# Gate and up matmuls from rounded halves, 384 columns at once, with rows stored modulated and the down step in two banks

## What is computed

```python
x = x + g1[:, None, :] * (mixed @ w_out[l])
h2 = modulate(rms_norm(x, norm2_g[l]), sh2, sc2)      # h * (1 + scale) + shift
x = x + g2[:, None, :] * hier_moe(h2, ...)
return rms_norm(x, final_g)
...
def expert_block(args):                               # 32 experts, two of them for each row
    tok, e = args
    xb = h_pad[tok]
    a = jax.nn.silu(xb @ w_gate[e]) * (xb @ w_up[e])  # 1024 -> 256
    return a @ w_down[e]                              # 256 -> 1024
```

## Time and profile before

| | us |
|---|---|
| three runs | 1996.19, 1997.77, 1998.21 (median 1997.77) |
| the profiled execution | 1996.46 |
| its span, first to last instruction | 1994.3 |
| TensorE busy | 1801.4 (90%) |
| VectorE busy | 1179.6 (59%) |
| ScalarE busy | 855.5 (43%) |
| mean granted TensorE clock | 0.950 of full speed |

### The profile page before, as it was taken

How to read it: one execution, slowest core, us unless ns; L and a number is a source line. 1 busy time by engine, 2 the same in 40 slices (tenths; PEclk the granted TensorE clock), 3 DMA queues, 4 the chain that set the end, 5 groups by cost and what they waited for, 6 DMA issues and landing times. The chain is left out here.

```text
span 1994.3 us, 26932 instructions
## 1 busy us (share of the span) xinstructions
PE 1801.4 (90%) x8988; PEld 1479.5 (74%) x8988; DVE 1179.6 (59%) x2009; ACT 855.5 (43%) x1520; POOL 855.5 (43%) x887
## 2 busy tenths in 40 slices
PE   2899999997999999999995999965999999999980
PEld 2677878774777777777784788855899898999970
DVE  4597989857666666666644656553444444444444
ACT  3535454326676777677684232311222222222114
POOL 0032314103888888888892111112343443434330
PEclk8899999996999999999997999976999999999995
DMA  7656565530000000000005343414888787878848
GB/s 282 197 143 192 168 181 158 147 102 0 6 9 6 9 8 6 9 9 6 11 9 199 126 158 137 148 43 163 248 248 252 231 248 245 248 236 239 242 94 337
DMA packets 216176, 274.28 MB, mean 138 GB/s; under 512 B 28469, under 2 KB 176144, under 8 KB 215834
## 3 DMA queue, kind: packets, MB, share of 16 engines
q1 hardware_dynamic: 193498, 220.59, 34.1%
q0 software_dynamic: 20224, 52.47, 10.4%
q10 hardware_dynamic: 2368, 0.17, 0.1%
HBM read 229.13 MB, written 60.82 MB: 145 GB/s over the span
## 5 line engine op out<-in xcount | busy, mean ns | idle before, releaser
L1212 POOL TENSOR_TENSOR plo<-KR,phi 128x512 fp32r<-128x512 f32 (+1 forms) x320 | 353.1, 1123 | 44.6 <-ACT KR L1171 44.4
L1020 DVE TENSOR_REDUCE cmax<-tbank 128x1 f32<-128x512 f32 (+2 forms) x320 | 193.3, 605 | 106.8 <-PE tbank L835 101.6
L1170 ACT ACTIVATE phi<-tbank 128x512 fp32r<-128x512 f32 (+1 forms) x320 | 170.9, 534 | 141.8 <-PE tbank L884 137.3
L387 PE MATMUL pbank<-hhi,wslhi 128*128 128x512 f32 x512 | 207.7, 406 | 8.5 <-DVE wsllo L440 8.5
L1946 DVE TENSOR_SCALAR xTe<-ebank,modcol 128x256 f32<-128x256 f32 (+1 forms) x128 | 53.6, 471 | 262.2 <-PE ebank L1864 137.8
L387 PE MATMUL pbank<-hhi,wsllo 128*128 128x512 f32 x512 | 201.5, 394 | 0.0
L387 PE MATMUL pbank<-hlo,wslhi 128*128 128x512 f32 x512 | 201.4, 393 | 0.0
L331 POOL DMA_DIRECT2D wmod<-in_w_ada x64 | 48.5, 758 | 308.2 <-DVE macc L519 297.9
L1886 PE MATMUL ebank<-xTe,wg 128*128 128x192 f32 x1024 | 174.8, 330 | 3.1 <-DVE ahi L1979 1.8
L1886 PEld LDWEIGHTS ebank<-xTe,wg 128*128 128x128 f32 x1024 | 170.9, 193 | 8.0 <-DVE ahi L1979 2.1
L1886 PE MATMUL ebank<-xTe,wu 128*128 128x192 f32 x1024 | 171.6, 326 | 0.0
(11 more groups left out here) (279 smaller groups left out, 3963.4 us busy)
## 6 DMA issues: line engine op xcount, KB each, us to landing
wg<-in_w_exp_gate SPq DMA_DIRECT2D x32, 1024.0 KB, 5.5
wu<-in_w_exp_up SPq DMA_DIRECT2D x32, 1024.0 KB, 8.9
wd<-in_w_exp_down SPq DMA_DIRECT2D x32, 1024.0 KB, 5.0
wraw<-in_w_in SPq DMA_DIRECT2D x60, 512.0 KB, 4.4
wmod<-in_w_ada POOLq DMA_DIRECT2D x64, 256.0 KB, 3.5
xt<-in_x SPq DMA_DIRECT2D x4, 2048.0 KB, 11.4
wada<-in_w_ada SPq DMA_DIRECT2D x4, 2048.0 KB, 19.7
mixed<-mix_dram SPq DMA_DIRECT2D x16, 512.0 KB, 4.3
```

The lines of the kernel that those rows point to most:

```text
L387: ins = pe.matmul(out, w[:, S % 3, k], h[:, n % 2, k], start=k == 0 and j == 0, stop=k == KD - 1 and j == 2)
L1020: W(ve.tensor_reduce(cmax[:, i % 2, n:n + 1], plain[:, chunk % 2, 0:w], AX.X, ALU.max), plain_read)
L1170: A(act.activation(step_of(phi, m), scores[:, m % 2, j * P:512], ACT.Exp), phi_done)
L1212: po.tensor_tensor(step_of(plo, m), step_of(probs, m), step_of(phi, m).bitcast(F32), ALU.subtract).then_inc(plo_done, 1)
```

## The change

Gate and up now also run on halves. ScalarE rounds each half of `wg` and `wu` to `ghi` (8 blocks of 128 columns, four such operations an expert), and VectorE subtracts it to `glo` (four of 1024 columns). The raw weights have one buffer each (`gu[:, 0]`, `gu[:, 1]`). The transposed rows are stored as two halves side by side: ScalarE copies the high one from PSUM, VectorE subtracts the rest. For each block TensorE multiplies `ghi` by both halves at once, 384 columns, and adds `glo` by the high half, 192 columns. So a bank holds two parts, which have to be added: ScalarE copies the low part, VectorE adds the other (`add_gate`, `add_up`, 384 columns each), and Silu then works from SBUF. Gate and up take four banks, so the down step has two: `down_first` and `down_rest` use the same two in turn, and outputs are scaled in halves of 512 columns. The low half of `wd` is made by VectorE, as before.

The rows `xs` are now stored with scale and shift applied (two operations of 1024 columns in place of one). The row vectors for this come from three broadcast loads of 512 KB on ScalarE's queue, four matmuls of 512 columns and three operations of VectorE; the one-column matmuls, the scaled router weights and the router's bias step go. The last stage scales each tile in place and stores two tiles (1 MB) at a time.

```diff
-                ve.tensor_scalar(xs[:, b], x2[:, b], xstat[:, b, 2:3], None, ALU.mult).then_inc(xs_ready, 1)
+                ve.scalar_tensor_tensor(xs[:, b], x2[:, b], xstat[:, b, 2:3], scrow[:], ALU.mult, ALU.mult
+                                        ).then_inc(xs_scaled, 1)
+                ve.wait_ge(xs_scaled, t + 1)
+                ve.tensor_tensor(xs[:, b], xs[:, b], shrow[:], ALU.add).then_inc(xs_ready, 1)
...
+            act.dma_start(shrow[:], b_ada[0, 3 * D:4 * D].partition_broadcast(P)).then_inc(ld_srow, 16)
+            act.dma_start(scrow[:], b_ada[0, 4 * D:5 * D].partition_broadcast(P)).then_inc(ld_srow, 16)
+            act.dma_start(xs[:, 1], T["norm2_g"][0, :].partition_broadcast(P)).then_inc(ld_srow, 16)
...
-        xT = sb("xTe", [P, KD, 2 * CAP])
+        xT = sb("xTe", [P, KD, 2, 2 * CAP], F32R)
...
-        wg, wu, wd = sb("wg", [P, 2, KD, FE]), sb("wu", [P, 2, KD, FE]), sb("wd", [P, 2, KF, D])
+        gu, wd = sb("gu", [P, 2, KD, FE]), sb("wd", [P, 2, KF, D])
+        ghi, glo = sb("ghi", [P, 2, KD, FE], F32R), sb("glo", [P, 2, KD, FE], F32R)
...
-        turn, gate, up, outa, outb = bank[:, 0:2], bank[:, 2], bank[:, 3], bank[:, 4:6], bank[0:CAPB, 6:8]
+        turn, gate, up, outp = bank[:, 0:2], bank[:, 2:4], bank[:, 4:6], bank[:, 6:8]
...
+            def load_gate(r, i, g):
+                sp.wait_ge(glo_ready, r * (NEXP * 4) + i * (NGRP * 4) + (g * 4 + 2))
+                sp.dma_start(gu[:, 0], wgd[:, bass.ds(i * KD + g * EPG * KD, KD), :]).then_inc(ld_g, 16)
+
+            def load_up(r, i, g):
+                sp.wait_ge(glo_ready, r * (NEXP * 4) + i * (NGRP * 4) + (g * 4 + 4))
+                sp.dma_start(gu[:, 1], wud[:, bass.ds(i * KD + g * EPG * KD, KD), :]).then_inc(ld_u, 16)
+
+            def load_down(r, i, g):
+                sp.wait_ge(dlo_ready, r * NEXP + i * NGRP + (g + 1))
+                sp.dma_start(wd[:, g % 2], wdd[:, bass.ds(i * KF + g * EPG * KF, KF), :]).then_inc(ld_wd[g % 2], 16)
...
-                        sp.wait_ge(up_done, r * NEXP + i * NGRP + (g + 1))
-                        sp.dma_start(wg[:, b], wgd[:, bass.ds(i * KD + g * EPG * KD, KD), :]).then_inc(ld_gu[b], 16)
-                        sp.dma_start(wu[:, b], wud[:, bass.ds(i * KD + g * EPG * KD, KD), :]).then_inc(ld_gu[b], 16)
-                        sp.wait_ge(dlo_ready, r * NEXP + i * NGRP + (g + 1))
-                        sp.dma_start(wd[:, b], wdd[:, bass.ds(i * KF + g * EPG * KF, KF), :]).then_inc(ld_wd[b], 16)
+                        load_up(r, i + (g + 1) // NGRP, (g + 1) % NGRP)
+                        load_down(r, i + (g + 1) // NGRP, (g + 1) % NGRP)
+                        load_gate(r, i + (g + 2) // NGRP, (g + 2) % NGRP)
...
-                for w, out, done in ((wg, gate, gate_done), (wu, up, up_done)):
+                pe.wait_ge(turn_dve, r * (PAIRS * 6) + q * 6 + (6 + b * 2))
+                for m, (out, free) in enumerate(((gate, gate_added), (up, up_added))):
+                    pe.wait_ge(free, r * NEXP + q * 2 + (b + 1))
                     for f in range(KF):
+                        pe.wait_ge(glo_ready, r * (NEXP * 4) + q * 8 + (b * 4 + m * 2 + f + 5))
+                        at, both = slice(f * P, (f + 1) * P), out[:, f, 0:2 * CAP].rearrange("p (h n) -> p h n", h=2)
                         for k in range(KD):
-                            ins = pe.matmul(out[:, f * CAP:(f + 1) * CAP], w[:, b, k, f * P:(f + 1) * P],
-                                            xT[:, k, cols_of[b]], start=k == 0, stop=k == KD - 1)
-                    ins.then_inc(done, 1)
-
-            def down(out, b, lo, hi, done):
+                            pe.matmul(both, ghi[:, m, k, at], xT[:, k, :, cols_of[b]], start=k == 0, stop=False)
+                            ins = pe.matmul(both[:, 0], glo[:, m, k, at], xT[:, k, 0, cols_of[b]],
+                                            start=False, stop=k == KD - 1)
+                        ins.then_inc(unit_done, 1)
...
+            def down(n, b, lo, hi, done):
+                out = outp[0:hi - lo, n]
                 for f in range(KF):
                     for j, (a, w) in enumerate(((ahi, dhi), (alo, dhi), (ahi, dlo))):
-                        for n in range(2):
-                            ins = pe.matmul(out[:, n], a[:, b, f, lo:hi], w[:, b, f, n * 512:(n + 1) * 512],
-                                            start=f == 0 and j == 0, stop=f == KF - 1 and j == 2)
+                        ins = pe.matmul(out, a[:, b, f, lo:hi], w[:, b, f, n * 512:(n + 1) * 512],
...
-                pe.wait_ge(ya_done, r * NEXP + q * 2 + (b + 1))
-                down(outa, b, b * CAPB, b * CAPB + P, down_a)
+                for n in range(2):
+                    pe.wait_ge(yb_done, r * (NEXP * 2) + q * 4 + (b * 2 + n + 1))
+                    down(n, b, b * CAPB, b * CAPB + P, down_a)
 
             def down_rest(q, b, r):
-                pe.wait_ge(yb_done, r * NEXP + q * 2 + (b + 1))
-                down(outb, b, 0 if b else P, CAPB if b else CAP, down_b)
+                for n in range(2):
+                    pe.wait_ge(ya_done, r * (NEXP * 2) + q * 4 + (b * 2 + n + 2))
+                    down(n, b, 0 if b else P, CAPB if b else CAP, down_b)
...
+            def split_in(q, b, r, m, f):
+                ve.wait_ge(ghi_ready, r * (NEXP * 4) + q * 8 + (b * 4 + m * 2 + f + 1))
+                at = slice(f * P, (f + 1) * P)
+                ve.tensor_tensor(glo[:, m, :, at], gu[:, m, :, at], ghi[:, m, :, at].bitcast(F32), ALU.subtract
+                                 ).then_inc(glo_ready, 1)
+
+            def add_gate(q, b, r):
+                ve.wait_ge(low_copied, r * (NEXP * 2) + q * 4 + (b * 2 + 1))
+                ve.tensor_tensor(sg[:], sg[:], gate[:, :, 0:CAP], ALU.add).then_inc(gate_added, 1)
...
-                ve.wait_ge(down_b, r * NEXP + q * 2 + (b + 3))
-                ve.wait_ge(st_yb[b], r * (PAIRS * 16) + q * 16)
-                ve.scalar_tensor_tensor(yb[:, b], outb.rearrange("p a n -> p (a n)"),
-                                        gate_b[:, bass.ds(r * 0 + q * 2 + b, 1)], g2row[0:CAPB], ALU.mult, ALU.mult
-                                        ).then_inc(yb_done, 1)
+                for n in range(2):
+                    ve.wait_ge(down_b, r * (NEXP * 2) + q * 4 + (b * 2 + n + 5))
+                    if n == 0:
+                        ve.wait_ge(st_yb[b], r * (PAIRS * 16) + q * 16)
+                    at = slice(n * 512, (n + 1) * 512)
+                    ve.scalar_tensor_tensor(yb[:, b, at], outp[0:CAPB, n], gate_b[:, bass.ds(r * 0 + q * 2 + b, 1)],
+                                            g2row[0:CAPB, at], ALU.mult, ALU.mult).then_inc(yb_done, 1)
...
+            def split_in(q, b, r, m, f):
+                if f == 0:
+                    hold(act, ld_u if m else ld_g, r * (NEXP * 16) + q * 32 + (b * 16 + 16), passed)
+                act.wait_ge(unit_done, r * (NEXP * 4) + q * 8 + (b * 4 + m * 2 + f + 1))
+                at = slice(f * P, (f + 1) * P)
+                act.activation(ghi[:, m, :, at], gu[:, m, :, at], ACT.Copy).then_inc(ghi_ready, 1)
...
-            for t in range(NT):
-                sp.wait_ge(normed, t + 1)
-                sp.dma_start(out_rows[t * P:(t + 1) * P, :], res[:, t % NR]).then_inc(st_out[t % NR], 16)
-            for r in range(NR):
-                sp.wait_ge(st_out[r], 16 * NT // NR)
+                    "(p q) d -> p q d", p=P)).then_inc(ld[i], 16)
+            for i in range(NL):
+                sp.wait_ge(normed, 2 * i + 2)
+                sp.dma_start(out_rows[2 * i * P:(2 * i + 2) * P, :].rearrange("(p q) d -> p q d", p=P),
+                             x2[:, 2 * i:2 * i + 2]).then_inc(st_out, 16)
...
-                if t >= NR:
-                    ve.wait_ge(st_out[t % NR], 16 * (t // NR))
-                ve.scalar_tensor_tensor(res[:, t % NR], x2[:, t], stat[:, t, 2:3], fgrow[:], ALU.mult, ALU.mult
+                ve.scalar_tensor_tensor(x2[:, t], x2[:, t], stat[:, t, 2:3], fgrow[:], ALU.mult, ALU.mult
```

More of the change, by code:

```diff
@@ L1398, in step, with modulation_rows @@
                     turn_x(t - 1, 1 - b)
-                if at == 1:
-                    pe.wait_ge(rbias_read, 1)
-            def modulation_rows(piece, first):
+            def modulation_rows(piece, first, to):
                 pe.wait_ge(ld_macc[piece], 16)
                 for n in range(2):
-                    ins = pe.matmul(turn[:, n], cst[:, C_ONE:C_ONE + P], macc[:, first + n], start=True, stop=True)
+                    ins = pe.matmul(to[:, n], cst[:, C_ONE:C_ONE + P], macc[:, first + n], start=True, stop=True)
                 ins.then_inc(mod_summed, 1)
[L1408 to L1417, removed]
-                    ins = pe.matmul(logit_bank, shift[:, k], wr[:, k], start=k == 0, stop=k == KD - 1)
-                ins.then_inc(rbias_done, 1)
             tiles(pe, step)
@@ L2037, in _ @@
                 n = 5
```

(31 more changed lines are left out.)

260 lines of the change are left out of this document (159 added, 101 removed).

## The result

The changed kernel is slower: 2008.86 us (median of nine runs, 2002.32 to 2011.83) against 1997.99 for the kernel before beside it; the ratio is 1.0053, with a 95% interval of 1.0043 to 1.0063. The prediction was 1941 us, 1926 to 1978. The profiled execution has a span of 2006.5 us, 12.2 more than before.

| place in the program | before, us | after, us | difference |
|---|---|---|---|
| start to the first gate matmul | 1382.2 | 1433.8 | +51.6 |
| from there to the last scaled output of the experts | 555.8 | 518.3 | -37.5 |
| from there to the end | 56.3 | 54.4 | -1.9 |

A forecast was written before the change was run, and what follows sets the result against it. TensorE was taken to bound the expert stage, VectorE close behind. Gate and up -61.4, waits +6, first and last pair +1, mixing 0, last stage -2 sum to -56.4 us: 1941 us, range 1926 to 1978.

The forecast's parts named there:

- The mixing stage: Stage before the experts: one more 1024-column VectorE operation a tile, hidden by TensorE; cost 0, ends -4 and +6 us.
- a mixing stage over 6 us longer: Named sign that the forecast is wrong: the stage before the experts growing by over 6 us.
- rival C: Expert stage: weights land later than 10.4 us, VectorE waits; 1972 us at 11.4, 2053 at 14; chance .11, .06 slower.
- Rival D: Expert stage: the new VectorE subtractions cost more than 1.228 us; at 2.0 the kernel takes 2025 us; chance .05.
- Gate and up: Expert stage: a wide and a narrow matmul take .177 + .0875 us, an expert 8.48 instead of 10.40; -61.4 us.
- rival A: Expert stage: weight loads .11 us apart bind, .287 us a pair of matmuls; gain 39 us, total 1958; chance .10.
- the +6 of waits: Expert loop: TensorE and VectorE wait for each other, .4 us a pair of experts over TensorE's sum; +6 us over 15 turns.
- VectorE: Expert loop: 29.4 us of work a pair of experts against TensorE's 30.6, busy 27 to 30; waits cost +6 us.
- Loads: Expert stage: single raw buffers leave time for a 10.4 us landing, longest median was 8.2; cost nothing.
- the sign that was named for rival C: Expert stage: ScalarE's rounding of gate weights waits for the load, VectorE for ScalarE, with a landing above 10 us.
- The last stage: Final stage: tiles written in place and stored 1 MB at a time; -2 us, ends -3 and +1.3.

The follow-up runs named there:

- the order mended: Changed kernel with VectorE's two small operations for the next tile's scale moved ahead of the two 1024-column operations on the stored row: 1947.46 us, ratio 0.9754 to before.

## Why the prediction was wrong, step by step

- **The mixing stage, forecast 0 (-4 to +6), was +51.6 up to the first gate matmul.** This is the step that failed, and it alone turned the sign. The sentence was: VectorE is busy 151 of 270 us, TensorE 245, "so TensorE hides it". A busy share over a stage says that VectorE has time, not that its next operation may be late. In its place the runs showed a chain without slack: VectorE's order, ScalarE's copy, the router's matmuls. The 1.75 us put into it came out at TensorE in full, and 1.6 us of slower clock with them, in tile after tile. The .35 us that the router's weight load waited for ScalarE stood in the trace of the kernel before and said that this chain ended last already. Who waits for what is queued behind the added operations was asked in the expert stage, not here. That the clock would follow was not thought of either. The prediction did name the sign, a mixing stage over 6 us longer; its .11 for a slower kernel stood on rivals C and D, and neither of them made it slower.
- **Gate and up, forecast -61.4, was about -41** (32 x (10.40 - 9.12)): the mechanism was right, the term mis-sized. The price of .177 was right for wide ones in a row, and that of .0875 for a narrow one behind a wide one; alternating, the two cost .285. That is rival A's price (.287), given a chance of .10, and by the rows its cause too, the spacing of the loads, though the .02 shows at the wide matmul, not at the narrow one. Rival A's total of 1958 leaves the +6 of waits out without saying so; with it the sum is 1964.
- **VectorE, forecast 29.4 us of work less some overlap and +6 us of waits.** Its busy time is 88% of 31.8, 28.1 us, inside the 27 to 30 that were named. The waits did not come: TensorE is busy for the whole window beside it. So nothing had to be added. Whether the waits would have come at the 30.6 us that were forecast for TensorE, no run shows.
- **Loads.** The gate weights land after 7.3 us at the median, under the 10.4 that were worked out, but this median hides two kinds: from 1476 us on every second gate load took 9.4 to 10.2 us, but for one, and the others 5.3 to 7.6, so half of them came within 1 us of that bound. ScalarE waited 94 us in all for gate loads, the sign that was named for rival C, mostly without VectorE waiting too. One was late: issued at 1762.26, landed after 13.7 us, in use at 1776.16. VectorE waited 2.30 us for it, and TensorE 1.6 for VectorE, the mechanism of rival C; that turn took 33.99 us instead of 31.80:

```profile
1777.25 1.23 DVE L1974 TENSOR_TENSOR glo<-gu,ghi 128x1024 fp32r<-128x1024 f32 x1 [2.30 <-ACT ghi L2150]
```

- **Rival D** is out: the subtraction in eight runs takes 1.214 us (mean of 128), less than the 1.228 of the earlier trace rows.
- **The last stage**, forecast -2, was -1.9.

With the order mended, the time is 1947 us, inside the range that was given: what was forecast is what the change does when its mixing stage doesn't lose. That the two are only 6 us apart is in part luck, since errors of both signs are in it: +20 us for the pairs of matmuls, against 6 us of waits that did not come and 5 us that this version gains up to the first gate matmul (1377.0 against 1382.2).

## What to carry to other kernels

Before an operation is called hidden, look at what stands behind it on its engine, and follow that to the engine that sets the time: if the chain has no slack there, the full duration of what is added comes out at the end. Short operations on which other engines wait belong ahead of long ones that only a store or a later stage needs. And price two alternating kinds of matmul as a pair, with the spacing of their weight loads in the sum, not each from a row of its own kind.

## What the runs showed of the hardware that was not expected

A wait of TensorE of 1.2 us ahead of 36-column matmuls was followed by a fall of the granted clock from 1.00 to .50 (2.4 to 1.2 GHz) in each tile, at a cost of 1.6 us; with a delay of .53 us it stayed at 1.00. Filling the gap with six matmuls of 36 columns (twelve records in the trace) did not prevent it, though TensorE's wait was .42 us then; seven matmuls of 512 columns did. So a TensorE that the profile shows as busy for most of such a stretch does not always keep its clock.
